# Gate and up of four feed-forward stages as a 2 by 2 block product with seven block multiplications

## What is computed

```python
def swiglu_ffn(x, norm, w_gate, w_up, w_down):
    h = rms_norm(x, norm)
    return (jax.nn.silu(h @ w_gate) * (h @ w_up)) @ w_down
...
        x = x + 0.5 * swiglu_ffn(x, ffn1_norm[l], ffn1_w_gate[l], ffn1_w_up[l], ffn1_w_down[l])
...
        x = x + 0.5 * swiglu_ffn(x, ffn2_norm[l], ffn2_w_gate[l], ffn2_w_up[l], ffn2_w_down[l])
```

## Time and profile before

| | us |
|---|---|
| median of 3 runs | 3299.75 |
| lowest, highest | 3296.97, 3300.28 |
| the profiled execution | 3301.67 |
| its span in the trace | 3299.9 |

### The profile page before, as it was taken

How to read it: one execution, slowest core, us unless ns; L and a number is a source line. 1 busy time by engine, 2 the same in 40 slices (tenths; PEclk the granted TensorE clock), 3 DMA queues, 4 the chain that set the end, 5 groups by cost and what they waited for, 6 DMA issues and landing times.

```text
span 3299.9 us, 37217 instructions
## 1 busy us (share of the span) xinstructions
PE 3233.1 (98%) x14818; PEld 2592.5 (79%) x14818; DVE 1740.4 (53%) x2835; ACT 1284.0 (39%) x1948; POOL 76.1 (2%) x153
## 2 busy tenths in 40 slices
PE   9999999999999999999999999999999998999997
PEld 7888777677888888888877677878888776878886
...
GB/s 147 96 96 90 101 106 71 89 78 90 95 92 101 93 96 93 102 96 96 94 114 71 90 84 71 102 84 107 96 96 90 103 67 69 64 88 102 96 93 74
DMA packets 285246, 303.99 MB, mean 92 GB/s; under 512 B 11408, under 2 KB 271888, under 8 KB 285072
## 3 DMA queue, kind: packets, MB, share of 16 engines
...
## 4 chain that ended last, share of the span: by engine, by line
PE 88%; DVE 7%; ACT 3%; issue 1%; DMA 1%; DVEq 0%; ACTq 0%
PE bank L218 87%; DVE k_sc L180 2%; DVE k_wl L170 1%; ACT k_sc L214 1%; PE bank L224 1%; ACT k_wh L214 1%; DVE k_sc L170 1%; ACT L208 1%; DVE k_sc L196 0%; DVE k_x L180 0%; DVE k_sc L184 0%; DMA k_raw<-in_ffn_w_gate 0%; DVE k_xl L170 0%; DVE k_cv L180 0%; DMA k_m1tt<-in_relT 0%
## 5 line engine op out<-in xcount | busy, mean ns | idle before, releaser
L170 DVE TENSOR_TENSOR k_wl<-k_raw,k_wh 128x1024 fp32r<-128x1024 f32 (+1 forms) x547 | 655.2, 1201 | 1115.6 <-ACT k_wh L214 1102.2
L218 PE MATMUL bank<-k_xh,k_wh 128*128 128x512 f32 x2376 | 956.3, 403 | 7.9 <-ACT k_wh L214 4.9
L214 ACT ACTIVATE k_wh<-k_raw 128x1024 fp32r<-128x1024 f32 (+1 forms) x547 | 564.3, 1036 | 964.1 <-PE bank L218 713.4
L218 PE MATMUL bank<-k_xl,k_wh 128*128 128x512 f32 x2376 | 927.7, 390 | 1.7 <-DVE k_xl L170 1.7
L218 PE MATMUL bank<-k_xh,k_wl 128*128 128x512 f32 x2376 | 928.2, 391 | 0.5 <-DVE k_wl L170 0.4
L218 PEld LDWEIGHTS bank<-k_xh,k_wh 128*128 128x128 f32 x2376 | 447.7, 188 | 119.2 <-issue 19.1
L218 PEld LDWEIGHTS bank<-k_xl,k_wh 128*128 128x128 f32 x2376 | 447.7, 188 | 96.9 <-issue 7.6
L218 PEld LDWEIGHTS bank<-k_xh,k_wl 128*128 128x128 f32 x2376 | 446.9, 188 | 96.2 <-DVE k_wl L170 1.6
L218 PE MATMUL bank<-k_Gb,k_wh 128*128 128x512 f32 x704 | 218.2, 391 | 0.0
L218 PE MATMUL bank<-k_Ga,k_wh 128*128 128x512 f32 x704 | 218.2, 391 | 0.0
L218 PE MATMUL bank<-k_uh,k_wh 128*128 128x512 f32 x512 | 207.3, 405 | 3.3 <-DVE k_sc L170 3.3
...
## 6 DMA issues: line engine op xcount, KB each, us to landing
k_raw<-in_w_in SPq DMA_DIRECT2D x153, 512.0 KB, 3.7
...
```

What stands on the lines that cost most here:

```text
L170: return q.op(lambda e: e.tensor_tensor(out, a, b, op), cost(out))
L214: return self.A.op(lambda e: e.activation(out, a, f, bias=bias, scale=scale), c)
L218: fn = lambda e: e.matmul(out, l, r, start=start, stop=stop, skip_group_check=True)
```

## The change

In the four stages of the table `STRASSEN` gate and up are one block product. The tokens are cut into two halves and the 1024 features into two halves, so x is A11, A12, A21, A22; the gate weight is B11 over B21 and the up weight B12 over B22. Seven block multiplications (P1, P6, P2, P7, P5, P4, P3, in this order; Winograd's form) take the place of eight. For that:

- sums of blocks of x, S1 to S4, are made and split on DVE and ACT (`scaled_blocks` makes S2 as tiles 4 to 7 of x come in, `other_sums` the rest), and sums of raw weight units, T1 to T4, on DVE (`pre` and `post` of a piece);
- the matmul is turned round: 128 tokens by 128 features of x are the stationary operand and 512 columns of weight the moving one (a stage is four blocks of 512 columns and two of 384), so results are token-major;
- products are accumulated into banks whose earlier content has been copied out before (`copies`, on ACT: "a" after P1, "b" after P6, "c" after P7); silu and the multiplication of gate by up are done token-major with r as a number for each partition (`norm_tok` makes it with small matmuls), and then 4 transposes for each of 22 groups of 128 columns bring the result back for the down product, which is done in three parts instead of two;
- there are nine more raw units (`k_xraw`) and one more pair for a split unit (`k_xwh`, `k_xwl`).

Stage one keeps its form, but two banks of the pool MB are lent to LIN while it runs, so it has six. Lines move by three: L214, L170, L175, L180 and L218 become L217, L173, L178, L183 and L221.

The core of the diff:

```diff
+XRAW = 9
+STRASSEN = ("n2_0", "n1_1", "n2_1", "nf2")
...
+    def split(self, i):
+        loads, pre, src, post, frees, kt, n, ext = self.plan[i]
...
+        for c in pre:
+            self.combine(c, n)
...
+        th = self.ac(self.ktok[src] + free, h, raw, ACT.Copy)
+        tl = self.tt(self.ktok[src] + free + [th], lo, raw, h.bitcast(F32), ALU.subtract)
...
     def whole_x(self, k, tok, gname, free):
 
         s, fs = self.take(self.SC)
-        if gname is not None:
+        if gname in STRASSEN:
+            self.scaled_blocks(k, [tok, self.t_vec] + list(free), gname)
+        elif gname is not None:
             self.ut[k] = self.scaled(k, [tok, self.t_vec] + list(free), gname)
             self.xread[k] = [self.ut[k][0]]
         ta = self.ac([tok] + fs, s, self.X[k], ACT.Square)
...
+    def pair_of(self, w, src, dst):
+        t1 = self.ac(w, dst[0], src, ACT.Copy)
+        return t1, self.tt(list(w) + [t1], dst[1], src, dst[0].bitcast(F32), ALU.subtract)
+
+    def scaled_blocks(self, k, w, gname):
+
+        c = VEC[gname][0]
+        g = lambda i: self.vec[:, c + i:c + i + 1]
+        h, lo = self.UF[k]
+        n = width(h)
+        x = self.X[k]
+        t1 = self.ac(w, h, x[:, 0:n], ACT.Identity, scale=g(k))
+        t2 = self.stt(list(w) + [t1], lo, x[:, 0:n], g(k), h.bitcast(F32), ALU.mult, ALU.subtract)
+        self.uf[k] = (t1, t2)
+        if k < 4:
+            return
+        j = k - 4
+        s, fs = self.take(self.SC)
+        s1, s2 = s[:, 0:256], s[:, 256:512]
+        xj = self.X[j]
+        ta = self.ts(fs + list(w), s1, x[:, 256:512], g(k), None, ALU.mult)
+        tb = self.stt([ta], s1, xj[:, 256:512], g(j), s1, ALU.mult, ALU.add)
+        tc = self.stt([tb], s2, xj[:, 0:256], g(j), s1, ALU.mult, ALU.subtract)
+        self.sx[("S2", j)] = self.pair_of([tc] + list(w), s2, self.SX["S2"][j])
+        self.sj[j] = (s, tc)
+
+    def other_sums(self, gname, free):
+        c = VEC[gname][0]
+        g = lambda i: self.vec[:, c + i:c + i + 1]
+        for j in range(4):
+            q, fq = yield from self.wait_slot(self.SC)
+            ta = self.ts(fq, q[:, 0:256], self.X[j][:, 256:512], g(j), None, ALU.mult)
+            tb = self.stt([ta], q[:, 256:512], self.X[j][:, 0:256], g(j), q[:, 0:256], ALU.mult, ALU.subtract)
+            self.sx[("S3", j)] = self.pair_of([tb] + free, q[:, 256:512], self.SX["S3"][j])
+            self.SC.put(q, [self.sx[("S3", j)][1]])
+            yield
+        for j in range(4):
+            s, t = self.sj[j]
+            self.sx[("S1", j)] = self.pair_of([t] + free, s[:, 0:256], self.SX["S1"][j])
+            yield
+        for j in range(4):
+            s, t = self.sj[j]
+            t = self.stt([t, self.sx[("S2", j)][1]], s[:, 256:512], self.X[j + 4][:, 0:256], g(j + 4), s[:, 256:512],
+                         ALU.mult, ALU.add)
+            self.sx[("S4", j)] = self.pair_of([t] + free, s[:, 256:512], self.SX["S4"][j])
+            self.SC.put(s, [self.sx[("S4", j)][1]])
+            yield
+
...
+    def product(self, bank, frees, xop, spec, w, first):
+
+        done = [None] * 2
+        for h in range(2):
+            i, wh, wl, th, tl = self.piece(*spec[h], 2, w, True)
+            for t in range(2):
+                for jj in range(2):
+                    j = 2 * h + jj
+                    self.until(lambda: self.block(xop, j) is not None)
+                    xh, xl, t1, t2 = self.block(xop, j)
+                    cols = slice(t * P, (t + 1) * P)
+                    o = bank[t][:, 0:w]
+                    self.mm(frees[t] + [th, t1], o, xh[:, cols], wh[:, jj, :], first and j == 0, False)
+                    self.mm([t2], o, xl[:, cols], wh[:, jj, :], False, False)
+                    tok = self.mm([tl], o, xh[:, cols], wl[:, jj, :], False, j == 3, inc=(jj == 1))
+                    if (h, t, jj) != (1, 1, 1):
+                        self.quantum(1)
+                done[t] = tok
+            self.release(i, tok)
+        self.quantum(1)
+        return done
+
...
+    def ffn_blocks(self, l, wg, wu, wd, gname, scale, nextg):
+
+        G = self.sb(f"g{gname}", 16 * T, F32R, at=self.phase)
+        gh = [G[:, (2 * i) * T:(2 * i + 1) * T] for i in range(8)]
+        gl = [G[:, (2 * i + 1) * T:(2 * i + 2) * T] for i in range(8)]
+        start = self.marks()
+        lent = [self.MB.free.pop() for _ in range(2)]
+        self.LIN.free += lent
+        self.open_pair(start)
+        self.bg.append(self.norm_tok())
+        self.bg.append(self.other_sums(gname, start))
+        blocks = [(c, 512) for c in range(0, 2048, 512)] + [(2048, 384), (2432, 384)]
...
+        def spec(b, name):
+            c, w = blocks[b]
+            key = lambda n, h: (gname, b, n, h)
+            ld = lambda n, h: (key(n, h), ((wg if n[2] == "1" else wu), l, ((0 if n[1] == "1" else 4) + 2 * h) * P, 2, c, w))
+            out = []
+            for h in range(2):
+                q = lambda *n: tuple(key(x, h) for x in n)
+                one = {
+                    "P1": ((ld("B11", h), ld("B12", h)), (), "B11", ((q("T1", "B12", "B11") + (ALU.subtract,) + q("B11")),), ()),
+                    "P6": ((ld("B22", h), (key("T2", h), None)), ((q("T2", "T1", "B22") + (ALU.subtract, None)),), "T2", (), ()),
+                    "P2": ((ld("B21", h),), (), "B21", ((q("T3", "B22", "B12") + (ALU.subtract,) + q("B12")),), ()),
+                    "P7": ((), (), "T3", ((q("T4", "B21", "T2") + (ALU.add,) + q("B21")),), ("T3", "T2")),
+                    "P5": ((), (), "T1", (), ("T1",)),
+                    "P4": ((), (), "T4", (), ("T4",)),
+                    "P3": ((), (), "B22", (), ("B22",)),
+                }[name]
+                loads, pre, src, post, frees = one
+                out.append((loads, pre, key(src, h), post, q(*frees)))
+            return out
+
+        def banks():
+            x = [self.take(self.LIN) for _ in range(2)]
+            return [a for a, _ in x], [f for _, f in x]
+
+        def copies(b, name, done):
+            w = blocks[b][1]
+            d = st[b]
+            out = []
+            for t in range(2):
+                s, fs = yield from self.wait_slot(self.SC)
+                out.append((s, self.ac([done[t]] + fs, s[:, 0:w], d["x"][t][:, 0:w], ACT.Copy)))
+            d[name] = out
+
...
+        def d3(b, done):
+            w = blocks[b][1]
+            y = st[b]["y"]
+            out = []
+            for t in range(2):
+                u, tb = st[b]["b"][t]
+                s, ts_ = st[b]["s1"][t]
+                ta = self.tt([done[t], tb], u[:, 0:w], y[t][:, 0:w], u[:, 0:w], ALU.add)
+                self.LIN.put(y[t], [ta])
+                th = self.stt([ta, ts_], u[:, 0:w], u[:, 0:w], rcol(t), s[:, 0:w], ALU.mult, ALU.mult)
+                self.SC.put(s, [th])
+                out.append((u, th))
+            while "h2" not in st[b]:
...
+            for q in range(nf):
+                i = (b % 2) * nf + q
+                bk, fb = yield from self.bank(toks)
+                for t, (u, th) in enumerate(out):
+                    tr_ = self.tr(fb + [th, self.t_const], bk[:, t * P:(t + 1) * P], u[:, q * P:(q + 1) * P], self.ident, inc=(t == 3))
+                yield
+                gt[i] = self.split_to([tr_], bk, gh[i], gl[i], gfree[b % 2])
+                self.MB.put(bk, [gt[i][1]])
...
+        def run(b, name):
+            w = blocks[b][1]
+            d = st[b]
+            if name == "P1":
+                d["x"], fr = banks()
+                done = self.product(d["x"], fr, "A11", spec(b, name), w, True)
+                self.bg.append(copies(b, "a", done))
+            elif name == "P6":
+                self.until(lambda: "a" in d)
...
+                y, fr = banks()
+                done = self.product(y, fr, "A12", spec(b, name), w, True)
+                self.bg.append(d2(b, y, done))
+            elif name == "P7":
...
+        run(0, "P1")
+        for b in range(nb):
+            run(b, "P6")
+            run(b, "P2")
+            if b and b % 2 == 0:
+                down(b // 2 - 1, False)
+            run(b, "P7")
+            run(b, "P5")
+            if b + 1 < nb:
+                run(b + 1, "P1")
+            run(b, "P4")
+            run(b, "P3")
+        self.close_pair()
+        down(nb // 2 - 1, True)
...
+        self.open_units(self.marks())
         self.linear("w_out", l, 0, 8, 0, D, lambda k: (self.XH[k], self.XL[k], mt[k][0], mt[k][1]),
                     self.add_x(nextg, self.marks(), 0.5))
...
         self.warm(4)
+        lent = [self.MB.free.pop() for _ in range(2)]
+        self.LIN.free += lent
         self.bg.append(self.start_x(names[0]))
...
+                args = (l, "ffn1_w_gate", "ffn1_w_up", "ffn1_w_down", f"n1_{l}", 0.5)
+                if l:
+                    self.ffn_blocks(*args, nx(3 * l + 1))
+                else:
+                    self.ffn(*args, f"a{l}", nx(3 * l + 1))
```

(8 more changed lines are left out.)

321 lines of the change are left out of this document (275 added, 46 removed).

## The result

| | us |
|---|---|
| median with the change, 4 runs | 3409.56 (3404.96 to 3411.89) |
| median before in the same comparison, 4 runs | 3299.41 (3296.97 to 3300.28) |
| ratio | 1.0331, interval 1.0318 to 1.0344 |
| the profiled execution, its span | 3404.96, 3403.1 |

The account below looks back on a forecast made before the run. TensorE's instruction stream bounds the kernel. Profiled 3301.7 us, minus 75.2 saved, plus 124.7 idle at starts, 11.6 slow clock, 4 for P7 and 3 behind stages, gives 3369.8; less 1.9 to the median, 3368, range 3330 to 3394.

Parts of the forecast that it names:

- slow clock behind it: After each start's idle stretch TensorE runs at a granted clock of 0.50: 2.9 us a start, 11.6 in all.
- transposes: On TensorE in changed stages, 22 groups of four transposes cost 0.44 us each, 9.7 a stage.
- norm: Norm product in each changed stage goes from 1.2 us to four matmuls of 32 columns, some 0.3.
- P7's wait: P7 stands behind copies "b" and T3's split: about 1 us a stage, 4 in all (0 to 12).
- The start of each stage: P6 waits for copies "a" queued behind the sums on ACT: TensorE idle 27.7, 35.5, 27.7, 33.8 us, sum 124.7.
- What is hidden: In steady 512-column blocks DVE's 37.2 us and ACT's 25.7 fit under TensorE's 39.9; raw loads carry the same bytes.
- The pace: On TensorE, each matmul of 512 columns takes 0.2268 us, the step between starts read at 100.13 to 107.84.
- The mixer or product behind a changed stage: It gets four tiles at once from the down product's last part, where it had two: 3 us in all.
- Six banks as nothing: Stage one's six banks bring 0 us, as its rows already run at the full pace.
- Rival two: Stage starts are short: P6 waits only for T2's splits, idle 11 us a start, total 3285; chance 0.07.
- Rival one: DVE sets the time of steady blocks, 0.5 to 1 us more a block: 3385 to 3392; chance 0.15.
- Rival three: In changed stages, matmuls of 384 columns cost as much as those of 512: 67 us more, 3435; chance 0.04.

Follow-up runs that it names:

- the first experiment on less work at the start: Changed kernel with S3 made as tiles come, S1 and S4 after P6, P2 ahead of P6 in block one, down-part, last-tile and mixer 1 edits: 3352.31 us, 1.0164.
- the last experiment: Changed kernel with plain first block, sums reordered, down-part, last-tile and mixer 1 edits, P1 ahead of the last two up units: 3266.79 us, 0.9905 of before.

## Why the prediction was right in its direction and too small

Distances of the starts of matmuls, four stages together, measured against the term of the sum:

| term | predicted | measured | difference |
|---|---|---|---|
| idle at the four starts | 124.7 | 121.5 | -3 |
| slow clock behind it | 11.6 | 13.3 | +2 |
| matmuls of 512 columns | 609.6 | 623 | +13 |
| matmuls of 384 columns | 238 | 237 | -1 |
| transposes | 38.8 | 32 | -7 |
| norm | 1.2 | 7 | +5.5 |
| P7's wait | 4 | 0 | -4 |
| down products | 0 | 23 | +23 |
| mixers behind | 3 | 17.8 | +14.8 |
| the rest | 0 | -8 | -8 |

The last row is what remains: ahead of n2_0 4.6 us went, behind the last matmul 0.9, and the four stages' gate, up and norm took 962 and not 958 us before. The differences add up to +35, and between the profiled executions the miss is 3404.96 − 3369.8 = 35.2. Terms that were too small by some 58 us stand against terms too large by some 23, so it is luck that the miss is not larger.

- **The start of each stage** was right: place, releaser, order of instructions, and to 0.4 us the length in the first three; in nf2 P1 itself was held up 3.6, and the sum of both waits is 2.1 under the 33.8 given. That the copies' place in the queue makes it, as the prediction argued from the order, holds in part: with the copies "a" first P6 still waited 14.4, where the prediction had 10 or so if a copy could pass, P7 waited 9.3 for the copies "b" behind the sums, and the time hardly changed (1.031 for 1.0331). The amount of work counts as it was summed (7.7 less stall for 7.1 less work). In the first experiment on less work at the start, with S1 and S4 behind both sets of copies and S3 made earlier, 17 to 22 us a start were still left; what took them away was a product to cover the chain.
- **"What is hidden" failed for the down product.** It put nothing down for it, spoke of its covering DVE, and of the loads said only that they carry the same bytes; when a unit comes free for the next load it left out. Measured are 23 us more: the four waits of transposes behind a late load, 13.2 from start to start; a granted clock of 0.50 for the 3.4 us behind three of them, some 5; short waits for weight splits in n1_1 and n2_1, 3.1; and a longer step behind each group of transposes, 2.9. At the full clock its matmuls kept their pace of 0.229. Moving the part by one product removed the long waits, though the mixers took back 7.7 of the 16.5 us.
- **The pace failed as a size.** 0.2268 was read in stage one and taken for all; four of the seven products ran at 0.233, and the mean was 0.232, which is the +13. For S2 and S3 the place of the stationary tile decides; for the other products, and why a place should cost 3%, nothing was tried.
- **"The mixer or product behind a changed stage", 3 us,** was mis-sized: mixer 1 took 14.8 more, 8.4 by the planner's other order and 6.4 at its start behind the four tiles that come at once, and the third mixer 3.0 more. The prediction had the four tiles and left out that the planner would reorder a stage that the change does not touch.
- **Six banks as nothing** was looked for at 100 to 108 us only; in the trace of that edit alone, 4 us of stage one's first part went. The time does not show it.
- **Rival two** (a start under 18.8 us) fell with the 27 to 35 us that each start took. **Rival one** (DVE sets steady blocks) did not happen: no wait for `k_wl` or `k_xwl` of that size in any block. **Rival three** did not either: 384 columns took 0.174 to 0.177.

The saving that the prediction counted can be had: with the stalls covered (the last experiment) block products for 2304 of the 2816 columns give 32 us over the kernel before. The edits for the down part, mixer 1 and the last tiles and stage one's six banks are in these 32 us too.
